# Narrower attention units, and new edges of the expert stage, in a two-block transformer kernel

## The reference, cut to what matters

```python
# first block, in each layer: sliding-window and forgetting attention, 4 heads each, head width 64
s = einsum("bnqhgd,bnkhd->bnhgqk", qb, kk) * dh ** -0.5       # two key tiles of 128 for each query tile
s = where(local_ok & blk_ok, s + bias, NEG_INF)               # first query tile: its own key tile only
...
s = where(kpos[None, :] <= qpos[:, None], s + (c_q - c_k), NEG_INF)   # forgetting attention: causal over 256 keys

# second block, behind its mixer
x = x + gt_m * rmsnorm(merged @ w_out, g_mix_post)
h2 = rmsnorm(x, g_ffn_pre) * (1 + sc_f) + sh_f
logits = h2 @ w_router + b_router
top_logit, top_e = lax.top_k(logits, 4)                       # of 32 experts
top_w = softmax(top_logit)
# per expert: a = clamped_swiglu(xb @ w_gate + b_gate, xb @ w_lin + b_lin); y = a @ w_down + b_down
x = x + gt_f * rmsnorm(ffn, g_ffn_post)
```

## Time and profile before

| | us |
|---|---|
| median of three runs | 2717.95 (2716.56 to 2719.3) |
| the profiled execution | 2717.71 |
| its span | 2715.9 |
| TensorE busy | 2504.6 (92% of the span) |
| VectorE busy | 1221.4 (45%) |
| ScalarE busy | 860.4 (32%) |
| GpSimd busy | 43.8 (2%) |
| expert stage | 1690 to 2703 |
| last normalisation and store | 2703 to 2716 |

### The profile page before, as it was taken

How to read it: one execution, slowest core, us unless ns; L and a number is a source line. 1 busy time by engine, 2 the same in 40 slices (tenths; PEclk the granted TensorE clock), 3 DMA queues, 4 the chain that set the end, 5 groups by cost and what they waited for, 6 DMA issues and landing times. The chain is left out here.

```text
span 2715.9 us, 33148 instructions
## 1 busy us (share of the span) xinstructions
PE 2504.6 (92%) x12924; PEld 1674.1 (62%) x12925; DVE 1221.4 (45%) x1956; ACT 860.4 (32%) x1388; POOL 43.8 (2%) x62
## 2 busy tenths in 40 slices
PE   7998999899899899989989998699999999999997
PEld 6787898688688889778877887333333333333332
DVE  5555755664664575666454463612212212222212
ACT  5445444443443544344344443100100100100101
POOL 0000000000000000000000002000000000000000
PEclk9999999899899999989999999699999999999999
DMA  8654343663664534376361224599999999999974
GB/s 322 243 171 156 125 139 117 249 235 137 243 236 141 171 125 127 115 265 235 120 180 63 70 86 145 248 421 429 429 428 428 429 429 428 428 429 428 429 333 196
DMA packets 113468, 687.31 MB, mean 253 GB/s; under 512 B 20673, under 2 KB 22097, under 8 KB 87793
## 3 DMA queue, kind: packets, MB, share of 16 engines
q1 hardware_dynamic: 105840, 656.47, 62.4%
q0 software_dynamic: 7520, 29.37, 3.1%
q10 hardware_dynamic: 2, 0.01, 0.0%
HBM read 683.70 MB, written 2.11 MB: 253 GB/s over the span
## 5 line engine op out<-in xcount | busy, mean ns | idle before, releaser
L2153 PE MATMUL ps<-wexp_all_second,con_all_whole 128*64 128x512 f32 x3168 | 705.4, 595 | 29.1 <-DMA wexp_all_second<-in_w_lin 28.7
L2153 PEld LDWEIGHTS ps<-wexp_all_second,con_all_whole 128*64 128x64 f32 x3168 | 220.5, 137 | 469.4 <-issue 395.7
L513 DVE TENSOR_TENSOR lo_first<-raw_first,hi_first 128x1024 fp32r<-128x1024 f32 x264 | 308.1, 1220 | 33.9 <-ACT hi_first L470 33.9
L243 PE MATMUL ps<-hi_first,h_hi_first 128*128 128x512 f32 x704 | 286.3, 407 | 23.3 <-DVE lo_first L513 23.3
L245 PE MATMUL ps<-hi_first,h_lo_first 128*128 128x512 f32 x704 | 280.6, 399 | 0.0
L244 PE MATMUL ps<-lo_first,h_hi_first 128*128 128x512 f32 x704 | 280.6, 399 | 0.0
L470 ACT CAST hi_first<-raw_first 128x1024 fp32r<-128x1024 f32 x264 | 260.0, 1055 | 12.4 <-DMA raw_first<-in_ffn_wgu 12.4
L243 PE MATMUL ps<-h_hi_first,w_hi_first 128*128 128x256 f32 x848 | 248.1, 293 | 3.5 <-DVE w_lo_first L969 3.3
L244 PE MATMUL ps<-h_lo_first,w_hi_first 128*128 128x256 f32 x848 | 239.3, 282 | 0.0
L245 PE MATMUL ps<-h_hi_first,w_lo_first 128*128 128x256 f32 x848 | 239.2, 282 | 0.0
L969 DVE TENSOR_TENSOR w_lo_first<-raw_first,w_hi_first 128x1024 fp32r<-128x1024 f32 x122 | 148.6, 1222 | 153.9 <-ACT w_hi_first L880 153.2
(11 more groups left out here) (431 smaller groups left out, 3381.8 us busy)
## 6 DMA issues: line engine op xcount, KB each, us to landing
wexp_all_second<-in_w_gate SPq DMA_DIRECT2D x64, 2048.0 KB, 23.0
wexp_all_second<-in_w_lin SPq DMA_DIRECT2D x64, 2048.0 KB, 25.6
wexp_all_second<-in_w_down SPq DMA_DIRECT2D x64, 2048.0 KB, 20.5
raw_first<-in_ffn_wgu SPq DMA_DIRECT2D x176, 512.0 KB, 5.2
raw_first<-in_w_mix SPq DMA_DIRECT2D x138, 512.0 KB, 3.4
raw_first<-in_ffn_wd SPq DMA_DIRECT2D x88, 512.0 KB, 5.2
raw_second<-in_w_mix SPq DMA_DIRECT2D x57, 512.0 KB, 3.4
wada_first<-in_w_ada POOLq DMA_DIRECT2D x48, 512.0 KB, 5.8
```

Source lines behind the costliest of these rows:

```text
L243: nc.tensor.matmul(out, w_hi, x_hi, start=start, stop=False, skip_group_check=True)
L513: nc.vector.tensor_tensor(lo[:, slot], raw[:, slot], hi[:, slot].bitcast(F32), ALU.subtract).then_inc(s[f"{kind}_lo"], 1)
L2153: mm = nc.tensor.matmul(dst[side(half), :], lhs(k), B.wexp[2 * "gld".index(kind) + part][:, k % 4, half * HALF:(half + 1) * HALF], start=( ...
```

## The change

1. A unit of the attention has a width of its own, 128 for the first query tile: one key tile in scores, table, maximum, exponential, transposes, copy and values. The second query tile and the second block's attention stay.
2. The bias table's five operations go from GpSimd to VectorE, each behind one of the last weight splits; their DMAs are issued right after the load of the last product's first weight tile.
3. At the end of the second mixer ScalarE does a Sqrt whose result nobody uses.
4. In the expert stage the residual's product with the gain is made before the root is there and beside the squares; gain and root of the second norm are applied in the other order; transposes, logits, and selection go tile by tile; the four largest come from VectorE's MAX (the eight largest of a row), and MATCH_REPLACE, which marks the first place of each of them. SyncE's loop waits for the experts' ends (`ends_ready`), not for the whole list.
5. The last normalisation is made inside the expert stage, without a stage boundary, again with an unused Sqrt first.

```diff
     def prob(self, u):
-        return self.B.prob[u % DEPTH_A][:, 0:self.width]
+        return self.B.prob[u % DEPTH_A][:, 0:self.wide(u)]
...
-        for j in range(self.width // P):
+        for j in range(self.wide(u) // P):
...
-                return nc.tensor.matmul(dst, z[lo:lo + HD, AQ + h // 2, qc * P:(qc + 1) * P], B.kdup[lo:lo + HD, h // 2, :],
+                return nc.tensor.matmul(dst, z[lo:lo + HD, AQ + h // 2, qc * P:(qc + 1) * P], B.kdup[lo:lo + HD, h // 2, 0:(qc + 1) * P],
...
-                              values=[B.vtok[:, t, P + h * HD:P + (h + 1) * HD] for t in range(TC)],
+                              values=[B.vtok[:, t, P + h * HD:P + (h + 1) * HD] for t in range(qc + 1)],
...
             for c in range(N_MERGE2 + SPLIT - 1, N_MIX2):
                 lower(c)
+                if c - (N_MERGE2 + SPLIT - 1) < 5:
+                    bias_part_dve(dve, nc, s, B, c - (N_MERGE2 + SPLIT - 1))
+            dve.wait_ge(s["b_part"], 5)
...
+            nc.scalar.activation(B.stats[:, 2, 3:4], B.stats[:, 1, 3:4], ACT.Sqrt).then_inc(s["std_ready"], 1)
...
-            sp.wait_ge(s["listed"], 1)
+            sp.wait_ge(s["ends_ready"], 1)
...
+            for n, t in enumerate((1, 0)):
+                if n:
+                    dve.wait_ge(s["squared"], 1)
+                tt(B.acc[:, t, :], mixed[t], B.rows[:, 0, :], ALU.mult).then_inc(s["tmp_ready"], 1)
...
+                stt(B.x[:, t, :], B.acc[:, t, :], B.stats[:, 3, t:t + 1], B.x[:, t, :], ALU.mult, ALU.add).then_inc(s["x_ready"], 1)
...
+            gained(0)
             rstd_dve(dve, nc, s, B, slice(TC, 2 * TC), 2 * TC, 2)
             dve.wait_ge(s["rstd_ready"], 2)
+            normalized(0)
+            gained(1)
+            normalized(1)
...
+                dve.wait_ge(s["logits"], t + 1)
+                ch.link(tt(B.lg[:, t, :], ps[:, t, 0:E], B.v2("b_router"), ALU.add))
+                ch.link(nc.vector.max(B.top[:, t, :], B.lg[:, t, :]))
+                ts(B.rmax[:, t:t + 1], B.top[:, t, 0:1], -1.0, None, ALU.mult).then_inc(s["max_ready"], 1)
+                ch.link(nc.vector.memset(B.top[:, t, TOPK:], ABSENT))
+                ch.link(nc.vector.match_replace(B.chosen[:, t, :], B.top[:, t, :], B.lgx[:, t, :], CHOSEN))
+                tt(B.sel[:, t, :], B.chosen[:, t, 0:E], B.lg[:, t, :], ALU.is_gt).then_inc(s["sel_ready"], 1)
...
+            for t in range(TC):
+                dve.wait_ge(s[f"added{t}"], total + 1)
+                tt(B.htok[:, t, :], B.acc[:, t, :], B.rows[:, 3, :], ALU.mult).then_inc(s["y_gained"], 1)
+            rstd_dve(dve, nc, s, B, slice(0, TC), 3 * TC, 3)
+            dve.wait_ge(s["rstd_ready"], 3)
+            dve.wait_ge(s["y_gained"], TC)
             for t in range(TC):
+                stt(B.x[:, t, :], B.htok[:, t, :], B.stats[:, 3, t:t + 1], B.x[:, t, :], ALU.mult, ALU.add).then_inc(s["x_done"], 1)
```

More of the change, by code:

```diff
@@ L578, in __init__, with wide @@
         self.score, self.turn_bank, self.out_bank = banks
+    def wide(self, u):
+        return self.units[u].get("width", self.width)
     def prob(self, u):
-        return self.B.prob[u % DEPTH_A][:, 0:self.width]
+        return self.B.prob[u % DEPTH_A][:, 0:self.wide(u)]
     def stat(self, u, j):
@@ L588, in pe_scores @@
             pe.wait_ge(self.s["max_ready"], u - 1)
-        self.units[u]["scores"](self.score(u)[:, 0:self.width]).then_inc(self.s["scores_ready"], 1)
+        self.units[u]["scores"](self.score(u)[:, 0:self.wide(u)]).then_inc(self.s["scores_ready"], 1)
     def pe_turn(self, pe, u):
@@ L644, in act_turned @@
             act.wait_ge(self.s["out_ready"], u - 1)
[L645 removed]
+        self.nc.scalar.copy(self.B.prob_t[:, u % 2, 0:self.wide(u)], self.turn_bank(u)[:, 0:self.wide(u)]).then_inc(self.s["probs_t_ready"], 1)
     def act_out(self, act, u):
@@ L680, in fox @@
                 return mm
-            units.append(dict(scores=fox, table=con("causal")[:, qc, :], sink=None,
-                              values=[B.vtok[:, t, P + h * HD:P + (h + 1) * HD] for t in range(TC)],
+            units.append(dict(scores=fox, width=(qc + 1) * P, table=con("causal")[:, qc, 0:(qc + 1) * P], sink=None,
+                              values=[B.vtok[:, t, P + h * HD:P + (h + 1) * HD] for t in range(qc + 1)],
                               out=B.fox_tok[:, qc, h * HD:(h + 1) * HD]))
@@ L1168, in bias_table_sp, with bias_part_dve @@
     sp.dma_start(B.bdown, I["bias_down2"]).then_inc(s["b_in"], 16)
[L1171 to L1182, removed]
+def bias_part_dve(dve, nc, s, B, n):
+    part = (n + 1) // 2
+    rest = slice(0, (3 - part) * E)
+    if n == 0:
+        dve.wait_ge(s["b_in"], 64)
+    else:
+        dve.wait_ge(s["b_part"], n)
+    if n % 2:
+        nc.vector.tensor_tensor(B.braw[rest], B.braw[rest], B.btri[rest], ALU.subtract).then_inc(s["b_part"], 1)
+    else:
+        nc.vector.tensor_copy(B.btri[rest], B.braw[rest]).then_inc(s["b_part"], 1)
 class Bufs:
@@ L2269, in _ @@
                 block_turn(j, False)
+            nc.scalar.activation(B.stats[:, 2, TC:TC + 1], B.stats[:, 1, TC:TC + 1], ACT.Sqrt)
+            for t in range(TC):
+                act.wait_ge(s[f"added{t}"], total + 1)
+                act.wait_ge(s["squared"], 2 * TC + t)
+                square_sums(nc, s, B, B.acc[:, t, :], t, 0)
+            rstd_act(act, nc, s, B, slice(0, TC), 3)
         @block.vector
@@ L2300, in _ @@
-            red(B.rmax, B.lg, AX, ALU.max, negate=True).then_inc(s["max_ready"], 1)
-            for t in range(TC):
-                other, this = bcast(B.lg[:, t, :], 1, E), bcast(B.lg[:, t, :], 2, E)
-                ch.link(tt(B.cmp, other, this, ALU.is_equal))
-                ch.link(tt(B.cmp, B.cmp, con("earlier"), ALU.mult))
-                ch.link(tt(B.cmp2, other, this, ALU.is_gt))
-                ch.link(tt(B.cmp, B.cmp, B.cmp2, ALU.add))
-                ch.link(red(B.sel[:, t, :], B.cmp, AX, ALU.add))
```

131 lines of the change are left out of this document (58 added, 73 removed).

## The result

The changed kernel took 2683.72 us (median, 2680.05 to 2686.95) against 2718.62 for the one before: ratio 0.9869, 95% interval 0.9851 to 0.9887. 2679.8 was forecast, in a range of 2669 to 2690. The profiled execution has a span of 2682.1 us instead of 2715.9.

A forecast was written before the change was run, and what follows sets the result against it. TensorE's own work was taken to bound the attention, TensorE and DMA alternately the expert stage, with gains at its ends. 2717.71 - 11 (attention) - 2.0 (second mixer's end) - 20.1 (router) - 4.85 (tail) = 2679.8 us, range 2669 to 2690.

The forecast's parts named there:

- The bound: First block's attention: TensorE runs without gaps after each stretch's first stall, so its own work bounds and fewer columns save time.
- The stage shifts as a whole: Expert stage: the weights' stream waits on TensorE's buffer releases, so time cut ahead of it comes off the end.
- Attention, -11: Both layers' first-token-tile units, half as wide: 5.5 us saved a layer, 11 in all, ends -4 and -14.
- The matmul terms: Narrower attention matmuls: 0.21 us saved per score matmul, 0.11 per transpose, 0.2 per value matmul; 5.0 a layer.
- the net effect of the stall: TensorE's 3.09 us wait for ScalarE's copy, each attention stretch: 1.0 us shorter, but 0.5 of matmul savings swallowed.
- End of the second mixer, -2.0: Bias table leaves GpSimd, so the next stage starts after TensorE's last product: 2.0 us saved, ends -1.0 and -2.2.
- the bound of 2.29: Second mixer: upper estimate, in us, for each of the five bias-table operations moved to VectorE.
- Router, -20.1 up to the counting: Expert stage's start: counting begins 20.6 us in instead of 40.74, ends -16 and -25.
- The rival in which the clock rises earlier: TensorE's clock rises within the router, some 5 us, or stays up in attention: 2675 us; chance 0.14 for both together.
- the rival "slower": First expert's block: the new rhythm leaves TensorE at 1.2 GHz, so a block's 21.4 us of matmuls doubles; chance 0.02.
- Tail, -4.85: Last normalisation, without stage boundary or table load and with an earlier gain product: 4.85 us saved, ends -4 and -6.
- Sum: Whole kernel: attention, second mixer's end, router and tail savings taken off 2717.71 us give 2679.8.

The follow-up runs named there:

- attn_only: The kernel before with only the narrower attention units of the change added: 2709.71 us, ratio 0.9962 to the kernel before.
- no_attn: The changed kernel with its attention units at full width again: 2693.23 us, ratio 0.9897 to the kernel before.
- warm_both: The changed kernel plus spare TensorE matmuls: 38 at the expert stage's start, three behind the logits, four behind the counting: 2676.85 us, ratio 0.9835 to before.
- bias_pool: The changed kernel with the bias table made by GpSimd again, its DMAs behind all weight loads: 2687.68 us, ratio 0.9876 to before.
- sqrt_late: The changed kernel without the two unused Sqrt: 2684.06 us, ratio 0.9864 to the kernel before.
- wide_select: The changed kernel with the four largest logits found again by comparing each with each: 2690.75 us, ratio 0.9885 to the kernel before.
- wide_scores: The changed kernel with the first token tile's score matmuls at 256 columns again, the rest still narrow: 2687.98 us, ratio 0.9880 to before.
- after_again: The changed kernel measured once more, without any edit: 2683.99 us, ratio 0.9866 to the kernel before.
- listed_wait: The changed kernel with SyncE's loop waiting for the whole list again: 2684.46 us, ratio 0.9873 to the kernel before.
- own_tail: The changed kernel with the last normalisation in a stage of its own again: 2688.90 us, ratio 0.9876 to the kernel before.
- warm_late: The changed kernel plus three spare TensorE matmuls between logits and selection wait, four between counting and gathering wait: 2682.08 us, ratio 0.9853 to before.

## Why the prediction came out right, point by point

- **The bound.** TensorE in the attention: shown, in that its intervals shrink as sized and the mixers of layer 2 with them, in attn_only, no_attn and the changed kernel. The stage shifts as a whole, since the weights' stream hangs on TensorE's releases: shown. Block by block, the changed kernel's scatters start 18.0 us earlier in the stage at the first block and 18.4 at the last; in warm_both the 10 us gained at the start are all there at the end.
- **Attention, -11.** Ratio and medians give -10.3 and -9.2, but the mixers of the changed kernel give -2.0 and -4.8, 6.8 together. The matmul terms were sized right, 5.1 against 5.0 in layer 2. Mis-sized was the net effect of the stall, forecast as +1.0 for its shortening less 0.5 swallowed, 0.5 gained in a layer. Measured is a loss of 0.2 in layer 2 (waits of 4.5, then 4.7 us) and of 2.0 in layer 1 (3.1, then 5.1), where TensorE's first wait was 1.5 longer besides.
- **End of the second mixer, -2.0.** Measured -2.2, and 2.4 by bias_pool. Three of the five VectorE operations cost 1.2, the other two 2.28, near the bound of 2.29, and no wait of TensorE for a split appeared.
- **Router, -20.1 up to the counting.** Measured -19.9, step by step at the places forecast. What failed is the step from there: "the stage shifts as a whole" left TensorE's clock out. The counting is 19.9 earlier, the gate matmuls start 19.4 earlier (31.4 us in instead of 50.8) and take 2.5 longer. The down matmuls of the first block, which had suffered in the profile of before, get 0.6 back, the operations just ahead of them 0.55, and the rest of the stage 0.3. From the stage's start to the last scatter it is -18.35. The rival in which the clock rises earlier did not happen in the changed kernel. Beside the work the clock rose later: in the middle of the gate matmuls, where before it had been up when they began. That is the mechanism of the rival "slower", inside one block only. What the clock is worth in the router was put at 5 us; warm_both shows 7.5 up to the gate matmuls and 2.5 in them.
- **Tail, -4.85.** Measured -4.7.
- **Sum.** -38 forecast. The profiled spans differ by 33.8: mixers -2.0 and -4.8, the three feed-forwards -0.7, 0.0 and -1.7, second mixer -2.2, expert stage -18.35, tail -4.7, and a start later by 0.6. Against the forecast the attention is 4.2 short, the expert stage 1.75 and the start 0.6; 2.4 came back by luck, from the feed-forwards, which nobody had forecast and no edit touches. Without them the median would have been nearer to 2686 than to 2684, still inside the range.

## What to carry to other kernels

When serial work is cut out of a stretch where TensorE idles, look at the granted clock behind the stretch as well: a term summed up to the next matmul's start leaves out how fast that matmul runs. Let spare matmuls in a wait last until the real work begins: here nothing was left of their effect behind a rest of 2.4 us, and all of it behind one of 0.2. A matmul's column saving can show in two intervals, its own and that of the matmul behind it: half of the second score matmul's 0.21 us was in the product behind. And a time near the forecast does not confirm its terms; the stage lengths showed one term 4 us short and another 2.4 us that belonged to none.

## What was not expected

Two patterns of the clock appear in the same instructions. The gate and down matmuls of the first block took 7.04 and 7.72 in before, 9.43 and 7.09 in attn_only, whose expert stage is the same code; of the kernels without spare matmuls, sqrt_late, bias_pool and wide_select had 7.03 or 7.04, wide_scores 8.22, the changed one, after_again, listed_wait, no_attn and own_tail 9.5 to 9.8. Each is one profile. The feed-forward behind the mixer of layer 2 took 204.0 to 204.2 us in some kernels and 205.4 to 206.4 in others, with the same 852 matmul records; here the changed kernel and own_tail:

```profile
1148.30:1352.42 204.12, 192.31 (x852) 157.87 (x852) 119.17 (x147) 86.39 (x115) 6.84 (x13) 0.97 0.59 206
```

```profile
1149.87:1356.15 206.28, 194.76 (x852) 159.82 (x852) 119.22 (x147) 86.39 (x115) 6.87 (x13) 0.96 0.58 204
```

VectorE's and ScalarE's time is the same, TensorE's differs by 2.4 us. Such jumps of 2 us come and go with edits elsewhere, and they are as large as several terms of the forecast; stage lengths tell the terms apart where medians can't. What sets the pattern stays open: no run varied it alone. Both profiles with wide units (before 205.8, no_attn 206.0) have the long feed-forward and most with narrow ones the short, but bias_pool, own_tail and warm_late have narrow units and 206.3 or 206.4, so the units' width does not settle it.
